# Scan opening and expert weight requests in another order

## What is computed

```
def step(S, inp):                      # wkv_scan, per direction and head
    r_t, w_t, k_t, v_t, a_t, b_t = inp # called with a = -kk, b = kk * a
    sa = einsum('bhij,bhj->bhi', S, a_t)
    S = S * w_t[..., None, :] + v_t[..., :, None] * k_t[..., None, :] + sa[..., :, None] * b_t[..., None, :]
    return S, einsum('bhij,bhj->bhi', S, r_t)
...
hid = silu(einsum('nd,edf->nef', xt, w1)) * einsum('nd,edf->nef', xt, w3)   # hier_moe: 16 experts, D_EXPERT 256
y = einsum('nef,efd->nd', hid * gate[..., None], w2)                        # two experts have a gate for each token
```

## Time and profile before

| what | us |
|---|---|
| median of three runs (1475.34 to 1478.3) | 1475.67 |
| the profiled execution | 1485.73 |
| its span, first to last instruction | 1483.9 |
| PE busy in the span | 1271.5 |
| DVE, ACT, POOL busy | 528.9, 339.2, 383.9 |
| mean granted PE clock, as a share of full | 0.928 |

### The profile page before, as it was taken

One profiled execution on the slowest core, in us unless ns is written; L12 is line 12 of the kernel. 1 busy time (PEld: TensorE's weight loads), 2 busy tenths in 40 slices (PEclk: granted clock), 3 DMA queues, 4 the chain that ended last, 5 costly groups with the idle time before them and its releaser, 6 DMA issues. The chain is left out here.

```text
span 1483.9 us, 22069 instructions
## 1 busy us (share of the span) xinstructions
PE 1271.5 (86%) x8819; PEld 883.9 (60%) x8819; DVE 528.9 (36%) x1169; ACT 339.2 (23%) x825; POOL 383.9 (26%) x710
## 2 busy tenths in 40 slices
PE   4899988999999997897687889799977876888887
PEld 2456856778887786354454545555865544545456
DVE  2530095556666664643310111500236233110115
ACT  2351163222222121222211111200145222111111
POOL 0100086445544441100132331000037200424210
PEclk9999988999999999798799999799979986999997
DMA  9852035667656514253499767593300444867652
GB/s 361 217 170 85 1 123 154 181 180 213 215 160 187 160 42 140 95 198 129 169 392 407 282 228 250 199 175 110 103 15 1 162 184 163 324 222 248 230 175 82
DMA packets 200709, 264.70 MB, mean 178 GB/s; under 512 B 93883, under 2 KB 155467, under 8 KB 184992
## 3 DMA queue, kind: packets, MB, share of 16 engines
q1 hardware_dynamic: 163200, 221.63, 44.5%
q0 software_dynamic: 17152, 31.20, 5.8%
q10 hardware_dynamic: 20256, 10.48, 3.4%
HBM read 300.11 MB, written 28.96 MB: 222 GB/s over the span
## 5 line engine op out<-in xcount | busy, mean ns | idle before, releaser
L2064 PE MATMUL psum<-ring,slab 128*64 128x256 f32 x896 | 191.4, 396 | 17.0 <-DMA slab<-moe_w,slab 12.3
L2064 PE MATMUL psum<-slab 128*64 128x256 f32 x832 | 172.2, 382 | 0.0
L2064 PEld LDWEIGHTS psum<-ring,slab 128*64 128x64 f32 x896 | 116.4, 143 | 75.7 <-issue 35.0
L2092 PE MATMUL psum<-ring,ws 128*64 128x512 f32 x224 | 105.7, 652 | 16.9 <-issue 15.0
L2064 PEld LDWEIGHTS psum<-slab 128*64 128x64 f32 x832 | 107.5, 138 | 3.6 <-issue 1.0
L2237 DVE TENSOR_TENSOR ws<-ws,psum 128x256 f32<-128x256 f32 (+1 forms) x28 | 16.9, 604 | 240.6 <-PE psum L2064 117.4
L2092 PE MATMUL psum<-slab,ws 128*64 128x512 f32 x208 | 99.1, 659 | 1.3 <-issue 1.3
L2308 PE MATMUL psum<-slab,ring 128*128 128x384 f32 x256 | 84.5, 494 | 7.2 <-PEq L176 7.2
L2156 POOL DMA_INDIRECT y_rows<-slab x26 | 26.4, 1014 | 248.3 <-DVE slab L2247 229.4
L2501 POOL TENSOR_SCALAR ws<-ws 128x384 f32<-128x384 f32 x32 | 39.4, 1243 | 190.4 <-DVE ws L2571 190.4
L1269 DVE TENSOR_TENSOR ws<-psum,causal 128x512 f32<-128x512 f32 x96 | 63.7, 686 | 47.5 <-PE psum L879 46.4
(11 more groups left out here) (368 smaller groups left out, 2441.3 us busy)
## 6 DMA issues: line engine op xcount, KB each, us to landing
ring<-moe_w SPq DMA_DIRECT2D x84, 1024.0 KB
ring<-ada_w SPq DMA_DIRECT2D x46, 1024.0 KB, 9.1
ws<-inverses SPq DMA_DIRECT2D x48, 256.0 KB, 3.8
slab<-moe_w SPq DMA_DIRECT2D x12, 1024.0 KB, 8.8
ring<-na_w_qkv SPq DMA_DIRECT2D x12, 1024.0 KB
slab<-y_rows SPq DMA_DIRECT2D x12, 512.0 KB, 6.6
ring<-rwkv_w_r SPq DMA_DIRECT2D x4, 1024.0 KB
ring<-rwkv_w_k SPq DMA_DIRECT2D x4, 1024.0 KB
```

Source lines behind the costliest of these rows:

```text
L2064: last = nc.tensor.matmul(k.psum[BT * g:BT * g + BT, h_bank(s, kind), 0:DE], cols_[s % 2][:, c, BT * g:BT * g + BT], w[g][:, c, :], start= ...
L2092: last = nc.tensor.matmul(k.psum[BT * g:BT * g + BT, 5 + half, :], turned_hid[s % 2][:, P * f + BT * g:P * f + BT * g + BT], w[g][:, f, 51 ...
```

## The change

In the scan's opening round 1's `rate` is made by DVE in place of POOL, `bands` of round 1 move from the opening into round 0 (between its first and second `pairs`), `modulate(0)` moves behind the casts and the turned states, `rows_copy(0)` behind round 1's exponentials, and DVE clears `ak` and `ab` and scales the states ahead of round 1's `scaled_ar` and `scaled_kb`. In both mixtures the overflow blocks are dealt over the pairs in the order 0, 10, 1, 9, 2, 8, 3, 7, 4, 6, 5; POOL asks for the next pair's w1 and w3 ahead of the last step's `put` and for its w2 behind it; and `last_rows` with DVE's copy moves from the phase's start to step 2.

```diff
-PAIR = [(0, 1), (2, 3)] + [(4 + j, NE + j) for j in range(OVER)] + [(NE - 1,)]
+SPACED = [j // 2 if j % 2 == 0 else OVER - 1 - j // 2 for j in range(OVER)]
+PAIR = [(0, 1), (2, 3)] + [(4 + j, NE + SPACED[j]) for j in range(OVER)] + [(NE - 1,)]
...
             rates_in(8, 12)
-            modulate(0)
             pe.wait_ge(kk_inverse, 2)
...
             last.then_inc(state_turned, 1)
-            for d in range(2):
-                pe.wait_ge(band_ok[d], 1)
-            for part in range(2):
-                bands(1, part)
+            modulate(0)
             pe.wait_ge(nkk_ok, DC)
...
+                if r == 0:
+                    for d in range(2):
+                        pe.wait_ge(band_ok[d], 1)
+                    for part in range(2):
+                        bands(1, part)
                 for d, b in enumerate(D2):
                     if d == 0 and r < MOD_PAIRS:
                         pe.wait_ge(sel_ok, r + 1)
...
             sigmoids(10, 16)
-            rows_copy(0)
...
                 exps(d, *place(1, d), (0, 2))
+            rows_copy(0)
             band_copy(1)
...
-                dve.wait_ge(rate_ok[d], r + 1)
+                if r == 1:
+                    dve.wait_ge(rate_late[d], 1)
+                else:
+                    dve.wait_ge(rate_ok[d], max(r, 1))
...
-            dve.wait_ge(nkk_ok, DC)
-            for d in range(2):
-                scaled_ar(d, 1)
-                scaled_kb(d, 1)
             dve.wait_ge(state_turned, 1)
+            for d in range(2):
+                dve.wait_ge(centred[d], 3)
+            for d, b in enumerate(D2):
+                nc.vector.memset(b.ak[b.late, :, :, :, b.early], 0.0).then_inc(y_ok[d], 1)
+                nc.vector.memset(b.ab[b.late, :, :, :, b.early], 0.0).then_inc(y_ok[d], 1)
             dve.wait_ge(edges_ok, 4)
...
+            dve.wait_ge(nkk_ok, DC)
             for d, b in enumerate(D2):
-                nc.vector.memset(b.ak[b.late, :, :, :, b.early], 0.0).then_inc(y_ok[d], 1)
-                nc.vector.memset(b.ab[b.late, :, :, :, b.early], 0.0).then_inc(y_ok[d], 1)
+                q, n, _ = place(1, d)
+                toks = bass.ds(P * n, P)
+                dve.wait_ge(z_read[d], len(Z))
+                dve.wait_ge(band_out[d], 32)
+                nc.vector.tensor_tensor(b.rate, k.act3(S_NKK)[:, bass.ds(2 * q, 2), toks], b.a[:, bass.ds(2 * q, 2), toks],
+                                        ALU.mult).then_inc(rate_late[d], 1)
+                scaled_ar(d, 1)
+                scaled_kb(d, 1)
...
                 pool.wait_ge(z_read[d], len(Z))
-                pool.wait_ge(first_ok[d], 2)
-                pool.wait_ge(band_out[d], 32)
-                rates(d, 1)
...
-                        pe.wait_ge(*((hid_ok, s) if s else (last_ok, 1)))
+                        if s:
+                            pe.wait_ge(*((last_ok, 1) if s == 2 else (hid_ok, s)))
...
-            last_rows()
             turn(0)
             for s in range(PAIRS):
+                if s == 2:
+                    pe.wait_ge(hid_ok, s)
+                    last_rows()
                 inner(s)
...
             for s in range(PAIRS):
+                more = 2 <= s + 1 < PAIRS - 1
+                if s + 2 < PAIRS:
+                    gather(s + 2)
+                if more:
+                    overflow(s + 1, range(2))
                 if s:
                     put(s - 1)
-                if s + 2 < PAIRS:
-                    gather(s + 2)
-                if 2 <= s + 1 < PAIRS - 1:
-                    overflow(s + 1)
+                if more:
+                    overflow(s + 1, range(2, 3))
```

More of the change, by code:

```diff
@@ L787, in phase_scan @@
     band_half, band_done = k.sem("scan_band_half"), k.sem("scan_band_done")
+    rate_late = pair("rate_late")
     BATCH = [(0, 2), (2, DC)]
@@ L1335, in _ @@
             divide(6, DC)
-            dve.wait_ge(nkk_ok, DC)
+            dve.wait_ge(state_turned, 1)
             for d in range(2):
-                scaled_ar(d, 1)
-                scaled_kb(d, 1)
-            dve.wait_ge(state_turned, 1)
+                dve.wait_ge(centred[d], 3)
+            for d, b in enumerate(D2):
+                nc.vector.memset(b.ak[b.late, :, :, :, b.early], 0.0).then_inc(y_ok[d], 1)
+                nc.vector.memset(b.ab[b.late, :, :, :, b.early], 0.0).then_inc(y_ok[d], 1)
             dve.wait_ge(edges_ok, 4)
@@ L2157, in put, with overflow @@
                                              ys[s % 2][0:n, :], None, bounds_check=2 * T - 1, oob_is_err=False).then_inc(y_out[s % 2], 16)
-            def overflow(s):
-                for kind in range(3):
+            def overflow(s, kinds):
+                for kind in kinds:
                     i = side_at(s, kind, 1)
@@ L2228, in _ @@
                                                ALU.mult, ALU.add).then_inc(spread_ok, 1)
-            dve.wait_ge(spread_turned, 1)
-            nc.vector.tensor_copy(by_row, k.psum[0:BT, 7, 0:T]).then_inc(last_ok, 1)
             for s in range(PAIRS):
                 n = parts(s)
+                if s == 2:
+                    dve.wait_ge(spread_turned, 1)
+                    nc.vector.tensor_copy(by_row, k.psum[0:BT, 7, 0:T]).then_inc(last_ok, 1)
                 dve.wait_ge(silu_ok, s + 1)
```

## The result

The changed kernel took 1439.65 us in the median (1436.92 to 1444.51, 4 runs) beside 1475.51 us (1471.76 to 1478.3, 4 runs) for the kernel before: a ratio of 0.9762, 95% interval 0.9728 to 0.9797. It is 36 us faster, where 8.4 were forecast, and far outside the range of 1460.5 to 1474. Its profiled execution took 1440.46 us, with a span of 1438.7 at a mean clock of 0.936.

The account below looks back on a forecast made before the run. PE bounds the kernel, held by a 6.0 us wait in the scan's opening and 12.3 us for overflow weights. Scan -2.2, mixtures -6.8 and -0.2, last rows +0.8 give -8.4: from 1475.67 to 1467.3 us, range 1460.5 to 1474.

Parts of the forecast that it names:

- POOL pays for no wait of PE: Mixtures: POOL's three requests, 1.3 us each, are issued before the step's outputs are ready for `put`, so PE waits for nothing.
- its ten steps take what the second's took: First mixture: without waits for weights, its steps 2 to 11 fall from 157.04 us to the second mixture's 150.25.
- the order's term: Mixtures: w1 and w3 are asked for some 9 us sooner; counted only through the weights' waits, with no other gain.
- First mixture's weights: First mixture: spaced overflow blocks and earlier requests end PE's waits for weights, 6.8 us of gain, from 3 to 10.
- Scan: Scan's opening: first level 3.9 us sooner, less 1.7 for the clock, net -2.2 us, from -5.5 to +1.
- ACT's wait: Scan's opening: PE newly waits some 1.8 us for ACT between round 1's bands and the second pairs.
- the inverses: Scan's opening: PE stands 3 us ahead of the first level, until the inverses land at 240.1, between 238.4 and 241.2.
- The clock's term: Scan's opening: PE's new waits let the clock fall for a stretch, costing 1.7 us, from 0 to 4.
- Last rows: Mixtures: `last_rows` gains 0 at the start and lies on PE's path at step 2, +0.8 us, from 0.4 to 1.7.
- Half clock in the opening: Rival, 14%: the clock falls ahead of the casts, first level 2.5 us later than before, scan +2.5, whole 1472.0.
- More steps with a fallen clock: Rival, 6%: the clock falls in more mixture steps at 1.7 us each; seven more make the kernel slower, 1479.
- The larger gain: Rival, 8%: the clock holds and the inverse lands early, -5.5 in the scan, -10 in the first mixture: 1461.

Follow-up runs that it names:

- e5: The changed kernel itself, run again: 1440.69 us beside 1487.46 for the kernel before, ratio 0.9679.
- e6: The changed kernel with the old order of POOL's requests: 1484.6 us beside 1487.46 for the kernel before, ratio 0.9973.
- e2: The kernel before with only the new pairing of overflow blocks: 1466.87 us beside 1468.63, ratio 0.9994.
- e1: The kernel before with only the new order of POOL's requests in the mixtures: 1447.86 us beside 1468.63, ratio 0.9871.
- e13: The kernel before with the new request order and pairing, without the scan and last-rows parts: 1441.09 us beside 1478.99, ratio 0.9739.
- e18: The changed kernel, run again: 1439.43 us beside 1476.12 for the kernel before, ratio 0.9767.
- e4: The kernel before with only `last_rows` moved to step 2: 1466.12 us beside 1468.63, ratio 0.9993.
- e12: The changed kernel with round 0's second pairs of direction 1 made twice more as filling: 1440.54 us beside 1486.5 for the kernel before, ratio 0.9704.
- e10: The kernel before with the next overflow block's first request moved to the end of the previous batch: 1478.69 us beside 1486.5, ratio 0.9942.
- e11: The kernel before with only the gather moved ahead of the store: 1456.11 us beside 1486.5, ratio 0.9802.
- e16: The kernel before with the overflow block's first request asked for a batch earlier, repeated: 1470.08 us beside 1478.99, ratio 0.994.
- e8: The kernel before, unchanged, run for its profile on that group's chip: 1488.82 us beside 1487.46.

## Why the prediction was wrong

**The step that failed** is this: "POOL pays for no wait of PE", and with it "its ten steps take what the second's took". I costed POOL's requests by what waits for their data and took 14.30 us, the shortest step in sight, for one with nothing in its way. It held 1.8 us of delay: the same step takes 12.48 us with the new order. The row that would have told stood in the text, PE's 1.39 us at L2079 in step 2, which I read only as what makes the clock fall. Its releaser, DVE's product, was itself late behind nothing that DVE does. So the order's term, costed at 0 apart from the weights, is most of the gain: 20.8 us alone beside runs whose profiles lack the delay, and in e5's group the changed kernel loses all but 2.9 of 47 us without it (e6 against e5). How much of the 36 us is the delay and how much the waits for requests isn't known, since before's profiled execution was 10 us longer than its timed ones.

**First mixture's weights, -6.8 (3 to 10).** Mis-sized and for the wrong reason in part. The pairing alone gave nothing measurable (e2). On top of the order it shortens the first mixture by 4 to 8 us (143.1 in e1, 134.6 to 139.3 in the four profiles of the changed kernel, 136.5 in e13). That is near the forecast, but "I expect no wait for weights" was wrong: 9.6 us remain in the profile after, 5.8 of them for w2, the one kind that is still asked for at its old place.

**Scan, -2.2.** The mechanism was right, 5.4 us for a forecast of 3.9, with ACT's wait (1.43 us for 1.8) and the inverses (1.51 for 3) as releasers as written. The clock's term was mis-sized: 1.7 (0 to 4), and it cost 5.5 in the first profile; as the first level's gain less that of the mark behind it, against the profile before, it was 0.8 us in e18 (5.8 and 5.0) and 7.1 in e6 (3.9 sooner, 3.2 later). The net at the mark went from 5.0 us sooner (e18) to 3.2 later (e6), and was within 0.2 in three of the six.

**Last rows, +0.8.** e4's median is 2.5 us lower, with an interval from 5 lower to 3 higher: not to be told from nothing.

**The rivals.** Half clock in the opening came true in half: not ahead of `modulate`, as it said, but behind the pairs. The clock fell behind those short waits in six profiles of six, much more often than the 14% that I gave. The Trainium skill (TensorE: Matmul & The Clock Gate, section "HAM oscillation — how this bites in real kernels") tells of a kernel in which every wait for a transfer between bursts of products throws the clock back; these six profiles agree, with waits of 1.1 to 3.2 us for the inverses, and e12, with 2.20 us and no fall, does not. More steps with a fallen clock was wrong in the direction: the falls went with PE's gap, from 4 of 10 steps in the second mixture to none. The larger gain was named with 8%, but from the scan and the weights, so it was no forecast of this.

**Not settled:** what a request holds. That it is the run's position is shown by e10 (more lead, same end, same delay) and e11 (an end 1.3 us earlier, 1.4 us less delay). ACT's silu, 3.35 us ahead of the turn and within the second request of its run in either kernel, isn't late, so not every signal is held; whether it matters which request of a run it falls to, no run tests. And it isn't known why the delay is there in the profiles of the first comparison's before and of e6 to e11 and e16, and not in those of e2 to e4. The medians of the kernel before fit: 1468.6 us beside e2 to e4, 1486.5 and 1487.5 beside e5 to e12, and 1475.5 to 1479.0 in the other three sets, where timed executions with and without the delay may be mixed. The Trainium skill (Perfetto Trace Analysis, section "Summary: the profiler window per engine type") says that a TensorE end in the profile is an estimate and the actual one hidden; by it the products themselves could end late as well as the signal. No run here tells these apart.

## What to carry to other kernels

Before taking the shortest step for the undisturbed one, account for each gap in it: if an engine starts late and the named releaser is not among its waits, look at what another engine ends about 1 us earlier. Requests that move nothing are not free: 22 of them here cost 14 us at a bad place, and one request taken out of a run of five, which then ended 1.3 us earlier at the spot where TensorE hands over to VectorE and ScalarE, gave 30 us with one moved line (e11). And time won ahead of a gap of TensorE is only won if the clock holds in it; look at the next fixed mark behind the gap, not at the mark that was improved.

## What the runs showed of the hardware

An indirect request takes 1.00 us on GpSimd with 0.30 to the next, whether it moves 1 MB or nothing. In five profiled kernels with a run of five near the hand-over (before, e6, e8, e10, e16) VectorE and ScalarE started 0.9 to 1.1 us after the run's end in most steps, in three (e2 to e4) at once.

The same kernel before had medians of 1468.6 to 1487.5 us in the groups, the changed one of 1439.4 to 1445.4: with the delay and its clock falls gone, most of the spread between groups went too.

POOL's copy of 128x256 numbers at 232.12 in the changed kernel took 2.00 us while DVE made its products, and 0.40 two copies later; the price of the two working at once was paid there and held nothing, since POOL's next work waited 3.63 us for PE. At the inverse's last product, where the forecast put 0.3 us, it was 0.04 (1.14 for 1.10).
